# Column sums of seven norms: seven squares in a running sum and the eighth summed on top in PSUM, in a two-block kernel on one core

## What is computed

```python
def rmsnorm(x, g):
    xf = x.astype(jnp.float32)
    y = xf * lax.rsqrt(jnp.mean(xf * xf, axis=-1, keepdims=True) + EPS)
    return (y * g.astype(jnp.float32)).astype(x.dtype)
```

## Time and profile before

| | us |
|---|---|
| median of 3 runs | 3428.24 |
| lowest, highest | 3427.46, 3431.59 |
| the profiled execution's own time | 3424.79 |
| span of the profile | 3423.1 |
| TensorE matmul busy | 3196.5 (93%) |
| VectorE busy | 1564.3 (46%) |
| ScalarE busy | 716.4 (21%) |

### The profile page before, as it was taken

One profiled execution on the slowest core, in us unless ns is written; L12 is line 12 of the kernel. 1 busy time (PEld: TensorE's weight loads), 2 busy tenths in 40 slices (PEclk: granted clock), 3 DMA queues, 4 the chain that ended last, 5 costly groups with the idle time before them and its releaser, 6 DMA issues.

```text
span 3423.1 us, 38425 instructions
## 1 busy us (share of the span) xinstructions
PE 3196.5 (93%) x16031; PEld 2511.1 (73%) x16031; DVE 1564.3 (46%) x2297; ACT 716.4 (21%) x1190; POOL 79.6 (2%) x147
## 2 busy tenths in 40 slices
PE   4899999996998998889999999989989999999997
PEld 3777865553655897678888888868758788888886
DVE  6435125624114556434433443469982544334335
ACT  3332235512112555411000000021141100000002
POOL 1000000100004000000000000000000000000000
PEclk7999999997898999799999999999989999999998
DMA  7001110012110000211111111101101111111111
GB/s 285 19 18 40 41 25 16 16 62 74 37 38 10 1 1 1 74 56 50 50 49 49 49 49 49 34 24 47 32 14 50 62 37 49 49 49 49 49 37 49
DMA packets 138667, 153.29 MB, mean 45 GB/s; under 512 B 27016, under 2 KB 126252, under 8 KB 137004
## 3 DMA queue, kind: packets, MB, share of 16 engines
q1 hardware_dynamic: 136704, 134.40, 12.5%
q10 hardware_dynamic: 1835, 17.11, 1.2%
HBM read 138.91 MB, written 12.58 MB: 44 GB/s over the span
## 4 chain that ended last, share of the span: by engine, by line
PE 55%; DVE 2%; ACT 1%; issue 0%; DMA 0%; DVEq 0%; SPq 0%; ACTq 0%
PE ps L1217 42%; PE ps L1194 10%; PE ps L1290 1%; PE ps L742 1%; DVE sc L2331 0%; PE ps L758 0%; PE ps L1327 0%; DVE h_low L2335 0%; DVE sc L1837 0%; DVE ht L1894 0%; DMA out_dram<-sc 0%; ACT big L1775 0%; ACT h_high L1793 0%; DVE big L2451 0%; ACT sc L1796 0%
## 5 line engine op out<-in xcount | busy, mean ns | idle before, releaser
L1217 PE MATMUL ps<-h_high,w_high 128*128 128x512 f32 x1408 | 549.6, 390 | 15.0 <-DVE h_low L2335 15.0
L1217 PE MATMUL ps<-h_low,w_high 128*128 128x512 f32 x1408 | 549.2, 390 | 0.0
L1217 PE MATMUL ps<-h_high,w_low 128*128 128x512 f32 x1408 | 549.1, 390 | 0.0
L1194 PE MATMUL ps<-h_high,ring_parts 128*128 128x512 f32 x1024 | 321.3, 395 | 23.3 <-DVE h_low L2335 9.3
L1217 PEld LDWEIGHTS ps<-h_high,w_high 128*128 128x128 f32 x1408 | 265.4, 188 | 70.7 <-issue 15.5
L1217 PEld LDWEIGHTS ps<-h_high,w_low 128*128 128x128 f32 x1408 | 265.4, 188 | 55.1
L1217 PEld LDWEIGHTS ps<-h_low,w_high 128*128 128x128 f32 x1408 | 265.2, 188 | 55.2
L1738 ACT ACTIVATE sc<-ps 128x1024 f32<-128x1024 f32 x44 | 45.3, 1029 | 1235.3 <-PE ps L1217 1235.3
L2311 DVE TENSOR_TENSOR xt<-ps,xt 128x1024 f32<-128x1024 f32 x176 | 211.7, 1222 | 146.9 <-PE ps L1217 146.9
L1217 PE MATMUL ps<-act_high,w_high 128*128 128x512 f32 x704 | 273.9, 389 | 0.0
L1217 PE MATMUL ps<-act_high,w_low 128*128 128x512 f32 x704 | 273.9, 389 | 0.0
(11 more groups left out here) (355 smaller groups left out, 4520.9 us busy)
## 6 DMA issues: line engine op xcount, KB each, us to landing
ring<-in_ffn_w_gate_dram SPq DMA_DIRECT2D x22, 1024.0 KB, 5.3
ring<-in_ffn_w_up_dram SPq DMA_DIRECT2D x22, 1024.0 KB, 5.3
ring<-in_ffn_w_down_dram SPq DMA_DIRECT2D x22, 1024.0 KB, 4.9
ring<-in_conv_w_pw_dram SPq DMA_DIRECT2D x24, 512.0 KB, 3.8
x_kept<-xt ACTq DMA_DIRECT2D x2, 4096.0 KB, 12.6
xt<-x_kept ACTq DMA_DIRECT2D x2, 4096.0 KB, 12.9
ring<-in_w_mod_dram SPq DMA_DIRECT2D x4, 1536.0 KB, 16.8
ring<-in_w_in_dram SPq DMA_DIRECT2D x10, 512.0 KB, 3.8
```

Source lines behind the costliest of these rows:

```text
L1194: last = mm(bank(banks + half), (hi, lo)[wp_][:, k, :], h_part[rp_][:, k, 512 * half:512 * half + 512], start=k == 0 and p_ == 0, stop=k = ...
L1217: return mm(o, w, rows, start=start and part_ == 0, stop=stop and part_ == 2)
```

## The change

In the seven plain norms VectorE no longer adds the last square (k = 7). TensorE waits for the running sum of squares 0 to 6 in `sc[:, 2, :]`, does its eight products on it, then waits for the last square in `sc[:, 1, :]` and does eight more, accumulated onto the same eight columns of PSUM. The semaphore counts follow: a plain norm counts `sq_used` up by 7 instead of 8, and two small functions give the counts at which a norm starts. The layernorm keeps its own work, with its counts renumbered. A wait of ScalarE on VectorE's count for the first two squares of a norm, which was always met, is left out.

```diff
+        def sq_made(n):
+            return 8 * (n - 0)
+        def sq_taken(n):
+            return 7 * n + (n > 5)
...
             def norm_sum(n):
                 if n in (1, 3, 6):
-                    pe.wait_ge(s.sq_ready, 8 * n + 7)
+                    pe.wait_ge(s.sq_ready, sq_made(n) + 7)
                     idle_products(4)
-                pe.wait_ge(s.sq_used, 8 * n + 8)
+                pe.wait_ge(s.sq_used, sq_taken(n) + 7)
                 for t in range(TB):
-                    last = mm(ps[:, 3072 + t:3073 + t], sc[:, 2, P * t:P * t + P], ones[:, 0:1], start=True, stop=True)
+                    last = mm(ps[:, 3072 + t:3073 + t], sc[:, 2, P * t:P * t + P], ones[:, 0:1], start=t == 0, stop=False,
+                              skip_group_check=True)
+                pe.wait_ge(s.sq_ready, sq_made(n) + 8)
+                for t in range(TB):
+                    last = mm(ps[:, 3072 + t:3073 + t], sc[:, 1, P * t:P * t + P], ones[:, 0:1], start=False,
+                              stop=t == TB - 1, skip_group_check=True)
                 last.then_inc(s.sum_done, 1)
...
             def square(n, k, src):
-                if 8 * n + k >= 2:
-                    a.wait_ge(s.sq_used, 8 * n + k - 1)
+                if k >= 2:
+                    a.wait_ge(s.sq_used, sq_taken(n) + k - 1)
...
             def sum_square(n, k):
-                if k == 0:
+                if k == 0 or k == KC - 1:
                     return
-                v.wait_ge(s.sq_ready, 8 * n + k + 1)
+                v.wait_ge(s.sq_ready, sq_made(n) + k + 1)
                 if k == 1:
                     tt(sc[:, 2, :], sc[:, 0, :], sc[:, 1, :], add).then_inc(s.sq_used, 2)
                 else:
-                    v.wait_ge(s.sq_used, 8 * n + k)
+                    v.wait_ge(s.sq_used, sq_taken(n) + k)
```

More of the change, by code:

```diff
@@ L1324, in _ @@
             for p_ in range(KC // 2):
-                pe.wait_ge(s.sq_used, 8 * 5 + 2 * p_ + 2)
+                pe.wait_ge(s.sq_used, sq_taken(5) + 2 * p_ + 2)
                 for t in range(TB):
@@ L1784, in _ @@
                 if k >= 2:
-                    a.wait_ge(s.sq_used, 8 * 5 + 2 * (k // 2))
+                    a.wait_ge(s.sq_used, sq_taken(5) + 2 * (k // 2))
                 f(planes(sc[:, k % 2, :]), zc[:, k], ACT.Square).then_inc(s.sq_ready, 1)
@@ L2443, in squares_added @@
             def squares_added(p_):
-                v.wait_ge(s.sq_ready, 8 * 5 + 2 * p_ + 2)
+                v.wait_ge(s.sq_ready, sq_made(5) + 2 * p_ + 2)
                 if p_ >= 2:
```

## The result

The changed kernel took 3435.84 us as the median of ten runs (3431.07 to 3442.18), against 3427.85 us of ten runs before (3423.07 to 3431.59). The ratio is 1.0027, with a 95% interval of 1.0018 to 1.0036: **slower by 8.0 us** by the medians (0.23%), 0.27% by the ratio, and clear of no change. The forecast was 8.7 us more, 3436.9 in 3432.0 to 3441.5. The profiled execution took 3431.07 us, the lowest of the ten, with a span of 3429.3, 6.2 us more than the span before.

The account below looks back on a forecast made before the run. TensorE was taken as the bound (busy 93%), with each norm a serial chain of waits. Norms 0, 1, 2, 3, 4, 6, 7 gave -0.95 + 1.47 + 2.15 + 1.97 + 1.1 + 1.9 + 1.05 = 8.7 us: 3436.9 us, range 3432.0 to 3441.5.

Parts of the forecast that it names:

- No cover: At the sums: running sum of seven and last square come together (2261.7, 2261.64), so both groups stand on the path.
- The price of a group: TensorE's added eight column sums per plain norm: 1.87 us at full clock, 3.55 at half.
- The dropped addition: VectorE's last addition before the sums: its removal takes 1.31 us out of the chain of waits.
- Norm 0: Sums start earlier, at 45.6, at half clock, and end at 52.7 against 53.65: 0.95 us less.
- Norms 1 and 3: Sums start where unread products end, both groups at full clock: column sums end 1.47 and 1.10 us later.
- Norm 1's spreading products: Products behind norm 1's sums: clock still full at 783, so they cost what they did before.
- Norms 4, 6 and 7: Clock falls during the sums, at the profile's moments: column sums end 1.1, 1.9 and 1.05 us later.
- The first rival: Added products keep the clock up through sums and spreading at norms 4 and 7: 3425.1 us, not slower; chance 0.06.
- All at half clock: Clock falls before the added groups at norms 1, 3, 4, 6, 7: 14.5 to 17 us more; chance 0.09.
- Cover by a late square: Last square late enough to hide the first group, each norm from 1 gaining up to 1.31 us: 3419.4; chance 0.02.

Follow-up runs that it names:

- experiment 3: Kernel before, VectorE's addition kept, with eight more unread products of the last square in each plain norm; 3450.41 us, ratio 1.0074.
- experiment 2: The change without its second group of products, so the last square is left out of the sums; 3417.18 us, ratio 0.9972 to the kernel before.
- experiment 1: Kernel before, with the eight column sums of a plain norm opened and closed as one accumulation; 3427.41 us, ratio 1.0002.
- experiment 4: The change in norm 0 alone, the other six plain norms as in the kernel before; 3427.10 us, ratio 0.9998.
- experiment 8: Kernel before, but at norms 4 and 7 VectorE's sum ends with the sixth square and TensorE sums three groups in a free bank; 3425.00 us, ratio 0.9991.
- experiment 5: Kernel before, with unread products of 448 columns also in front of the sums of norms 2, 4 and 7; 3419.98 us, ratio 0.9983.
- experiment 6: Kernel before, with the edits of experiment 4 and experiment 5 together; 3425.90 us, ratio 0.9984.
- experiment 9: Experiment 6 plus wide unread products behind the spreading of norms 3, 4, 5 and 6; 3421.57 us, ratio 0.9985 to the kernel before.

## Why the prediction was right

- **No cover.** The step that carried it, that the running sum of seven and the last square come at the same moment, held: no second group waited, and experiment 3 priced a group on the path at 1.80 and 3.40 us, with 23.4 us over seven norms.
- **The price of a group.** Taken as 1.87 at full clock and 3.55 at half; measured 1.80 and 3.41, so both were a little high.
- **The dropped addition** is on the path: experiment 2 gains 9.8 us by it. I had taken 1.31 us of it at norms 2, 4 and 7, and the rows of idle time say 1.33.
- **Norm 0** gained 1.05 us against 0.95.
- **Norms 1 and 3.** The sizes were off. The columns' end came 1.12 and 0.75 us later, where I had 1.47 and 1.10. I let the first group start where the unread products end; at norm 1 it starts 0.16 us earlier (775.66, while they end at 775.82), with its first weight load under them (775.28), and the two groups took 3.63 us together in place of my 3.82. The Trainium skill (TensorE: Matmul & The Clock Gate, "Part 2: What happens when you issue a matmul") says that TensorE's queue pulls weight loads ahead of products still running; the trace agrees, by the load at 775.28.
- **Norm 1's spreading products** were a miss of another kind. I had them at full clock, as before, because the clock was still full at 783 in the one profile; in the changed kernel it fell at 781.05, and they took 2.66 us in place of 2.05. The two errors at norm 1 nearly cancel: 1.12 + 0.61 = 1.73, where I had 1.47. At norm 3 they did slip behind the fall as forecast and took 3.68 us, forecast 3.79; but in the old form of experiments 1 and 4 they had taken 2.05 us and not 2.92, so that against those norm 3 costs 2.38 us and not 1.51.
- **Norms 4, 6 and 7** came to 0.13, 0.43 and 0.86 in place of 1.1, 1.9 and 1.05. The mis-sized term is the moment of the fall, which I had taken from the one profile: it came 3.8, 4.7 and 3.0 us behind the last square's start in the changed kernel, and 2.84, 3.75 and 2.71 before. In the first experiment, with the old form, it came at 3.66, 5.15 and 3.87. The prediction named this as what moves each norm by a microsecond either way. That the total came so near, 8.0 measured and 8.7 forecast, is in part luck: the distances of the changed kernel are 5.7 us longer than in one old execution and 8.7 longer than in the other, and outside the norms executions differ by as much.
- **The first rival** (the added products keep the clock up) is out: it fell during the second group at norms 4, 6 and 7, and the time is 8 us above before. Nor did the idle time before the sums decide it: in experiment 8 at norm 4 there was none, and the clock fell 5.1 us into products of one column, while behind the wide ones of experiment 5 it stayed full through the sums. The Trainium skill (TensorE: Matmul & The Clock Gate, "Why this matters for your kernels") has the rule of continuous work that the prediction cites; by it the time would have come to 3425.1, and in this case it did not hold for products of one column. **All at half clock** did not happen to the sums of norms 1 and 3, though it did to the spreading products of norm 3, and in part to those of norm 1. **Cover by a late square** did not either: a second group never waited.

## What to carry to other kernels

Before moving a VectorE addition into TensorE's accumulation, compare when the two operands are ready: if they come together, the extra group is paid in full (here 1.8 or 3.4 us for eight float32 products of one column, against 1.3 us for the addition). What pays is to hand over an operand that is ready while TensorE idles, as in experiment 8. The lowest median among the kernels that compute the whole norm is of one that leaves VectorE's additions alone and puts wide unread products ahead of the sums: experiment 5, 0.17% faster than the kernel before, and faster than the changed one by 0.44%, both by the ratios. Experiments 6, 8 and 9 cannot be told from it by their ratios.

## What the runs showed of the hardware

- In the layernorm 14 us of products of one column followed each other at a granted clock of 0.50 without its rising. In experiment 8 the clock fell at 2267.98, after 5.1 us of them without a gap behind the last large product. The wide ones did otherwise: six products of 448 columns in front of norm 2, after 19.65 us of idleness, ran while the clock rose, 2.03 us before the last square began (experiment 5).
- The fall of the clock is not tied to the kernel's own work to better than about a microsecond: behind the same instructions at norm 4 it came at 2.84 and 3.66 us. Executions of one kernel differ by up to 10 us (3417.9 to 3428.3 in experiment 5), so that a median of ten runs can sit in either of two clusters. Part of such a difference can come from the clock in stages that an edit does not touch: 0.97 against 0.80 over the same 20 us in experiments 5 and 6. The distances inside the norms told more than the times did.
